# Up projections that sum both activation halves into the same 256 PSUM columns

## What is computed

```
# block 1: gated, with a 3-tap convolution along the sequence, D_FF = 5632
h2 = rmsnorm(x, norm_ffn[l])
u = h2 @ w_up[l]                      # 256 x 2048 @ 2048 x 11264
up = jnp.pad(u, ((0, 0), (1, 1), (0, 0)))
u = up[:, :-2] * cw[0] + up[:, 1:-1] * cw[1] + up[:, 2:] * cw[2] + conv_b[l]
gate, val = jnp.split(u, 2, axis=-1)
x = x + (jax.nn.silu(gate) * val) @ w_down[l]
...
# block 2: square of a relu, D_FF_2 = 8192
# u = rms_norm(x) @ w_up_2 ; act = relu(u) ** 2 ; y = act @ w_down_2
```

## Time and profile before

| | |
|---|---|
| timed runs | 2583.70, 2588.72, 2589.14 us; median 2588.72 us |
| profiled execution, first to last instruction (span) | 2586.3 us |
| PE busy | 2532.6 us (98%) |
| DVE, ACT busy | 1524.2 us (59%), 1224.6 us (47%) |

### The profile page before, as it was taken

One profiled execution on the slowest core, in us unless ns is written; L12 is line 12 of the kernel. 1 busy time (PEld: TensorE's weight loads), 2 busy tenths in 40 slices (PEclk: granted clock), 3 DMA queues, 4 the chain that ended last, 5 costly groups with the idle time before them and its releaser, 6 DMA issues.

```text
span 2586.3 us, 32846 instructions
## 1 busy us (share of the span) xinstructions
PE 2532.6 (98%) x12492; PEld 2125.8 (82%) x12492; DVE 1524.2 (59%) x1719; ACT 1224.6 (47%) x1540; POOL 49.7 (2%) x71
## 2 busy tenths in 40 slices
PE   7999999999999999999999999999899999999997
PEld 6888888878888888888877887788788888888886
DVE  4665656655776467756765346655565565565555
ACT  5444456544655355534544344444544343443443
POOL 0100100000000000000000000000000000000000
PEclk9999999999999999999999999999999999999999
DMA  7665455655555555555546455445465555555553
GB/s 257 192 194 178 150 168 167 224 176 180 181 182 191 189 185 190 184 195 181 192 163 235 144 168 159 155 151 175 146 196 194 181 192 190 186 185 192 182 205 114
DMA packets 249926, 469.96 MB, mean 182 GB/s; under 512 B 22320, under 2 KB 25648, under 8 KB 249184
## 3 DMA queue, kind: packets, MB, share of 16 engines
q1 hardware_dynamic: 249824, 468.58, 55.2%
HBM read 466.42 MB, written 2.13 MB: 181 GB/s over the span
## 4 chain that ended last, share of the span: by engine, by line
PE 96%; DVE 2%; ACT 1%; issue 0%; DMA 0%; POOL 0%; SPq 0%; POOLq 0%; DVEq 0%; ACTq 0%
PE psum L1580 21%; PE psum L1542 19%; PE psum L1544 19%; PE psum L1543 19%; PE psum L1581 10%; PE psum L1584 1%; PE psum L1657 1%; PE psum L1670 1%; PE psum L1593 1%; PE psum L1583 1%; PE psum L1642 1%; PE psum L1819 1%; DVE wl L1012 0%; DMA raw<-in_w_in 0%; ACT wh L613 0%
## 5 line engine op out<-in xcount | busy, mean ns | idle before, releaser
L1012 DVE TENSOR_TENSOR wl<-raw,wh 128x1024 fp32r<-128x1024 f32 x856 | 1048.9, 1226 | 966.4 <-ACT wh L613 961.3
L613 ACT ACTIVATE wh<-raw 128x1024 fp32r<-128x1024 f32 x856 | 904.1, 1058 | 1046.0 <-PE psum L1544 621.6
L1542 PE MATMUL psum<-wh,ha 128*128 128x512 f32 x1728 | 697.1, 403 | 8.9 <-DVE wl L1012 8.5
L1544 PE MATMUL psum<-wh,ha 128*128 128x512 f32 x1728 | 676.4, 391 | 0.0
L1543 PE MATMUL psum<-wl,ha 128*128 128x512 f32 x1728 | 674.8, 391 | 0.0
L1580 PE MATMUL psum<-ha,wh 128*128 128x512 f32 x1320 | 465.9, 398 | 5.0 <-DVE x_rows L1221 4.5
L1542 PEld LDWEIGHTS psum<-wh,ha 128*128 128x128 f32 x1728 | 325.9, 189 | 76.0 <-issue 10.7
L1544 PEld LDWEIGHTS psum<-wh,ha 128*128 128x128 f32 x1728 | 325.4, 188 | 70.8
L1543 PEld LDWEIGHTS psum<-wl,ha 128*128 128x128 f32 x1728 | 326.1, 189 | 66.2
L1581 PE MATMUL psum<-ha,wl 128*128 128x256 f32 x1320 | 370.1, 280 | 0.0
L1580 PE MATMUL psum<-hb,wh 128*128 128x512 f32 x960 | 339.4, 398 | 5.2 <-DVE rows L1520 3.2
(11 more groups left out here) (211 smaller groups left out, 1416.2 us busy)
## 6 DMA issues: line engine op xcount, KB each, us to landing
raw<-in_w_up SPq DMA_DIRECT2D x152, 1024.0 KB, 5.0
raw<-in_w_in SPq DMA_DIRECT2D x120, 1024.0 KB, 5.1
raw<-in_w_down SPq DMA_DIRECT2D x108, 1024.0 KB, 4.9
raw<-in_w_out SPq DMA_DIRECT2D x32, 1024.0 KB, 5.0
raw<-in_w_branch_a SPq DMA_DIRECT2D x8, 1024.0 KB, 5.0
raw<-in_w_branch_b SPq DMA_DIRECT2D x8, 1024.0 KB, 4.9
x_rows<-in_x SPq DMA_DIRECT2D x4, 512.0 KB, 9.4
bias<-in_b_rpb SPq DMA_DIRECT2D x32, 64.0 KB, 6.8
```

What stands on the lines that cost most here:

```text
L613: act.activation(wh[q % SPLIT_SLOTS][:], raw[q // 2 % RAW_SLOTS][:, 2 * (q % 2):2 * (q % 2) + 2, :], ACT.Copy).then_inc(hi_done, 1)
L1012: dve.tensor_tensor(wl[q % SPLIT_SLOTS][:], raw[q // 2 % RAW_SLOTS][:, 2 * (q % 2):2 * (q % 2) + 2, :], wh[q % SPLIT_SLOTS][:].bitcast(F32 ...
L1542: pe.matmul(acc, hi, wh[s][:, c, :], start=first and c == 0, stop=False)
L1544: ins = pe.matmul(acc, lo, wh[s][:, c, :], start=False, stop=last and c == 1)
```

## The change

Each couple becomes three matmuls of 256 columns into the same 256 sums: hi weights x high activations, hi weights x low activations, lo weights x high activations. Two groups of channels share a bank, so a channel block needs 2 banks and a pair needs 4 (banks 0 to 3 for all channel blocks). Down passes use banks 4 to 7, but for the third one of block 1, which stays in banks 0 to 3. The copy of the left halves on ACT is gone; DVE takes the sums out and scales them in one instruction (in block 2 with the relu in it), and the square is an instruction of its own. PE no longer waits for `row_free` before later up passes, nor for the copy of the 1/rms row before the second channel block, nor for `chan_free` before the down passes other than that third one.

```diff
+    def half_bank(ffn, v):
+        return 2 * (1 - v) if ffn == 1 else 2 * v
+
+    def half(ffn, v):
+        b = half_bank(ffn, v)
+        return psum[:, b:b + 2, :].rearrange("p b (d s) -> p (b d) s", s=SEQ)
+
+    def row_bank(g):
+        high = R_DOWN1[0] <= g < R_DOWN1[2] or g >= R_DOWN2[0]
+        return (4 if high else 0) + 2 * (g % 2)
...
# ACT, up1_stage (the later stages move up by one)
-            if j == 0:
-                act.wait_ge(sem["cmask_in"], 4)
-                act.wait_ge(mm_done, S_UP1[p] + 8 * v + 8 + 16 * i)
-
-                act.activation(u_pad[v][:, :, 1:SEQ + 1], psum[:, 4 * v:4 * v + 4, 0:SEQ], ACT.Copy
-                               ).then_inc(sem["half_ok"], 1)
-            if j == 2:
-                act.wait_ge(sem["u_scaled"], v + 1 + 2 * pair)
+            if j == 1:
+                act.wait_ge(chan_free, FREE + 2 * pair + v + 1)
...
# DVE, up1_stage
             if j == 0:
-                dve.wait_ge(sem["half_ok"], count)
-                u = u_pad[v][:, :, 1:SEQ + 1]
-                dve.tensor_tensor(u, psum[:, 4 * v:4 * v + 4, SEQ:2 * SEQ], u, ALU.add).then_inc(chan_free, 1)
-            if j == 1:
-                dve.wait_ge(chan_free, FREE + count)
+                dve.wait_ge(mm_done, S_UP1[p] + 8 * v + 8 + 16 * i)
                 dve.wait_ge(sem["rstd_row_ok"], 1)
-                u = u_pad[v][:, :, 1:SEQ + 1]
-                dve.tensor_tensor(u, u, rstd_row[:].unsqueeze(1).to_broadcast([P, 4, SEQ]), ALU.mult
-                                  ).then_inc(sem["u_scaled"], 1)
+                dve.tensor_tensor(u_pad[v][:, :, 1:SEQ + 1], half(1, v),
+                                  rstd_row[:].unsqueeze(1).to_broadcast([P, 4, SEQ]), ALU.mult
+                                  ).then_inc(chan_free, 1)
...
# PE, channel_step
                 for d in range(4):
-                    acc = psum[:, 4 * v + d, :]
                     hi, lo = (w[s][:, c, P * d:P * d + P] for w in (wh, wl))
-                    if k < KC - 1:
-                        pe.matmul(acc, hi, both, start=k == 0, stop=False)
-                        ins = pe.matmul(acc[:, 0:SEQ], lo, src[:, k, 0, :], start=False, stop=False)
-                    else:
-                        pe.matmul(acc[:, 0:SEQ], lo, src[:, k, 0, :], start=False, stop=False)
-                        ins = pe.matmul(acc, hi, both, start=False, stop=True)
+                    pe.matmul(acc[:, d, :], hi, src[:, k, 0, :], start=k == 0 and d % 2 == 0, stop=False,
+                              skip_group_check=True)
+                    pe.matmul(acc[:, d, :], hi, src[:, k, 1, :], start=False, stop=False, skip_group_check=True)
+                    ins = pe.matmul(acc[:, d, :], lo, src[:, k, 0, :], start=False, stop=k == KC - 1,
+                                    skip_group_check=True)
...
# PE, channel_blocks and first_pair
-            pe.wait_ge(row_free, FREE + rows_before)
             with pe.Fori(0, n) as i:
...
-            pe.wait_ge(row_free, FREE + rows_before)
+            pe.wait_ge(row_free, FREE + rows_before - 1)
...
-            row_of_roots(count)
-            pe.wait_ge(sem["rstd_row_ok"], count)
+            row_of_roots(ffn)
+            pe.wait_ge(row_free, FREE + rows_before)
```

More of the change, by code:

```diff
@@ L800, in up1_stage @@
                 ins.then_inc(sem["conv_mid"], 1)
-            if j == 5 and v == 0:
+            if j == 4 and v == 0:
                 act.wait_ge(sem["conv_done"], 1 + 2 * pair)
                 act.activation(conv[0][:], conv[0][:], ACT.Silu).then_inc(sem["silu_done"], 1)
-            if j == 6 and v == 1:
+            if j == 5 and v == 1:
                 act.wait_ge(sem["act_ready"], pair + 1)
@@ L831, in tail @@
                 if b == 0 and j < 4:
-                    for stage in ((0, 1), (2, 3), (4, 5), (6,))[j]:
+                    for stage in ((0, 1), (2, 3), (4,), (5,))[j]:
                         up1_stage(p, stage, 1, j0 + n - 1, n - 1)
@@ L965, in up2_stage @@
         def up2_stage(j, c, i):
[L967 to L971, removed]
+            if j == 2:
                 act.wait_ge(sem["act_ready"], 11 + c + 1 + 4 * i)
@@ L1219, in evac @@
                 d = dst[:, :, bass.ds((b + m * i) * COLS, COLS)]
+                acc = psum[:, row_bank(g):row_bank(g) + 2, :]
                 if add:
-                    dve.tensor_tensor(d, psum[:, 2 * (g % 2):2 * (g % 2) + 2, :], d, ALU.add).then_inc(row_free, 1)
+                    dve.tensor_tensor(d, acc, d, ALU.add).then_inc(row_free, 1)
                 else:
-                    dve.tensor_copy(d, psum[:, 2 * (g % 2):2 * (g % 2) + 2, :]).then_inc(row_free, 1)
+                    dve.tensor_copy(d, acc).then_inc(row_free, 1)
             return evac
@@ L1259, in up1_stage @@
                     dve.wait_ge(sem["tap_done"], count)
-                tap = 0 if j == 3 else 2
+                tap = 0 if j == 2 else 2
                 for s in range(4):
@@ L1264, in up1_stage @@
                                                    par[:, bass.ds(w, 1)], conv[v][:, s, :], ALU.mult, ALU.add)
-                ins.then_inc(sem["tap_done" if j == 3 else "conv_done"], 1)
-            if j == 5 and v == 1:
+                ins.then_inc(sem["tap_done" if j == 2 else "conv_done"], 1)
+            if j == 4 and v == 1:
                 dve.wait_ge(sem["conv_done"], count)
@@ L1477, in up2_stage @@
             if j == 0:
-                dve.wait_ge(sem["usum_done"], c + 1 + 4 * i)
-                dve.tensor_tensor(u_sum[:], psum[:, 4 * (c % 2):4 * (c % 2) + 4, SEQ:2 * SEQ], u_sum[:], ALU.add
-                                  ).then_inc(chan_free, 1)
+                dve.wait_ge(mm_done, S_UP2[0] + 8 * (c % 4 + 1) + 64 * (c // 4) + 64 * i)
+                dve.wait_ge(sem["rstd_row_ok"], 2)
+                dve.scalar_tensor_tensor(u_sum[:], half(2, c % 2), 0.0,
+                                         rstd_row[:].unsqueeze(1).to_broadcast([P, 4, SEQ]), ALU.max, ALU.mult
+                                         ).then_inc(chan_free, 1)
             if j == 1:
                 dve.wait_ge(chan_free, FREE + C_UP2[0] + c + 1 + 4 * i)
[L1483 to L1490, removed]
+                dve.tensor_tensor(u_act[:], u_sum[:], u_sum[:], ALU.mult).then_inc(sem["act_ready"], 1)
+            if j == 3:
                 dve.wait_ge(sem["hb_hi"], 11 + c + 1 + 4 * i)
@@ L1751, in _ @@
             if p == 0:
-                first_pair(S_UP1[0], C_UP1[0], ha, T_FFN1, 1, rows_before, last_group)
-            channel_blocks(S_UP1[p] + 16 * peeled, C_UP1[p] + 2 * peeled, n - peeled, ha, rows_before)
-            pe.wait_ge(chan_free, FREE + C_UP1[p] + 2 * n - 1)
+                first_pair(1, S_UP1[0], C_UP1[0], ha, T_FFN1, R_DOWN1[0], last_group)
+            channel_blocks(1, S_UP1[p] + 16 * peeled, C_UP1[p] + 2 * peeled, n - peeled, ha)
+            if p == 0:
+                pe.wait_ge(sem["rstd_row_ok"], 1)
+            if p == 2:
+                pe.wait_ge(chan_free, FREE + C_UP1[p] + 2 * n - 1)
             enter = next_input(T_MIX2, R_DOWN1[p])
             def down_hook(b, j):
-                if p == 2 and b:
-                    if b == 1 and j == 1:
-                        pe.wait_ge(chan_free, FREE + 22)
+                if b == 0 and j == 2 * n - 1:
+                    pe.wait_ge(chan_free, FREE + 22)
+                if b:
                     enter(b, j)
             row_blocks(S_DOWN1[p], R_DOWN1[p], 4, 2 * n, hb, hb_by(j0, 4), extra=down_hook if p == 2 else None)
-            rows_before = R_DOWN1[p] + 4
         def four_transposes(bank, src, rows=P):
```

35 lines of the change are left out of this document (17 added, 18 removed).

## The result

The changed kernel takes 2596.72 us (median of nine runs, 2593.68 to 2598.61), the kernel before 2587.92 us (nine runs beside it, 2582.98 to 2589.14). The ratio is 1.0038, with a 95% interval of 1.0029 to 1.0047: slower by 0.4%. The prediction was 2596, slower.

A forecast was written before the change was run, and what follows sets the result against it. PE was taken to bound the kernel, busy 2532.6 of 2586.3 us. Terms +19.5 - 10.9 - 1.3 = +7.3 us give a span of 2593.6; with the median 2.4 us above the span, 2596 us, range 2576 to 2622.

The forecast's parts named there:

- Three matmuls for two: In the up passes, three matmuls of 256 take 360 ns against 352 for a couple, over 2432 couples: +19.5 us.
- The seam: Where chunk 14 meets chunk 15, two matmuls of 256 follow each other, starting 120 ns apart; the forecast took this price.
- The waits: PE's removed stops: -10.9 us ahead of up passes and -1.3 us for the 1/rms row.
- rival D: At heads of up passes a late split or evacuation catches PE and the 12.2 us stay: 2608 us; chance 0.1.
- The down passes: PE has no wait for the activation chain in a down pass; its shortening means nothing gained, nothing lost.
- B: In the up passes each matmul pays the slower beat's 16.6 ns: stream +43.8 us, kernel 2620 us; chance 0.2.
- C: In channel_step splitting a 512 costs nothing: the stream stays at 856 us, the waits are gained, 2576 us; chance 0.2.

The follow-up runs named there:

- the split alone: The kernel before with only its couples made three matmuls of 256 columns; banks, waits and evacuations as before: 2606.37 us, ratio 1.0079.

## Why the prediction was right

**The path.** PE bound the kernel and still does, and the work that DVE and ACT lost does not shorten it.

**Three matmuls for two, +19.5 us forecast.** 360.0 ns a place as forecast. Without the slow starts the second stretch before had 351.5 ns and all couples about 351.8, so the term is 8.2 x 2432 = +19.9 us. Alone on the chip it is 2606.37 - 2586.91 = +19.5 by the medians, and 17 to 24 by the interval of the ratio. The step that carried it was to take the price of a matmul from distances over many of them (226.7 for a 512, 346.9 for a couple at the faster beat) and not from the rows of the 256s inside couples. The seam at the earlier trace rows gave the same 120 and was the only direct sight of it.

**The waits, -12.2 us forecast.** By the profile: five heads at 1.98 - 0.22 = 1.76 us, the first at 1.71 - 0.23 = 1.48, two roots at 1.08 - 0.36 = 0.72, and the slow starts behind the six heads, 0.1 each. Behind the row of roots a slow start is left: the first 256 takes 0.20 us instead of 0.12. That makes 8.8 + 1.5 + 1.4 + 0.6 = 12.3 us less. Put back on the chip the waits cost 11.9. PE is not caught late in an up pass, so rival D was wrong.

**The down passes: a step that was wrong by 0.8 us.** The prediction says that PE has no wait for the activation chain in a down pass and that nothing is lost there. The kernel before has one, the 4.1 us for `hb` shown above. The third down pass of block 1 follows three pairs and not four and has six steps in a block, so PE comes to the last activations after 11.06 us, while they are ready 15.18 us after the up pass has ended. In the changed kernel the chain is a stage shorter, and they are ready after 16.00 us. DVE's rows in the two kernels show where it waits:

```profile
1302.14 1.22 DVE L1012 TENSOR_TENSOR wl<-raw,wh 128x1024 fp32r<-128x1024 f32 x1
1304.37 1.68 DVE L1263 SCALAR_TENSOR_TENSOR conv<-u_pad,par,conv 128x256 f32<-128x256 f32 x4 [1.01 <-ACT conv L798]
```

```profile
1310.30 1.23 DVE L1016 TENSOR_TENSOR wl<-raw,wh 128x1024 fp32r<-128x1024 f32 x1 [3.10 <-ACT wh L627]
1311.44 3.37 DVE L1265 SCALAR_TENSOR_TENSOR conv<-u_pad,par,conv 128x256 f32<-128x256 f32 x8
```

The up pass ended at 1297.25 and at 1303.49, so the taps of the convolution begin 7.12 us behind it before and 7.95 us now. In the changed kernel they stand behind a split in DVE's program, and that split waits 3.10 us for ACT, which works on `conv` first. All ten profiles with the old evacuation have 15.2 us here, all four with the new one 16.0. The wait costs more than its length, in either kernel: in the 4.1 us behind it the granted clock was 0.59 of full speed before and 0.50 now, and the row matmuls that run at the lower of the clock's two levels start 0.43 us apart instead of 0.23. Up to the next up pass the two profiles differ by only 0.07 us (557.73 and 557.80), a stretch that varies between 554.1 and 557.8 in the profiles of these kernels, so the 0.8 us do not stand out in it.

**The sum.** The first two terms give +7.6; the medians differ by 8.8 and the spans by 9.5. Of the last 2 us, 0.6 were there before the first up pass began (622.09 - 1.48 = 620.61 before, 621.20 after), and 0.9 in the first up pass of block 2 (93.4 us became 95.6, where 256 places and the removed waits account for 1.3). No run takes these apart, and the runs of one kernel differ by 5 us. That the time itself was met within 0.7 us is in part luck: the forecast started from a median of 2588.7 us, and nine runs have 2587.92.

**The rivals.** B's slower beat did not appear: all streams of 256s ran at 120.0 ns, and only streams that change width showed it. C's point, that a 512 splits for nothing, is refuted by the split alone. The 109 ns that it cited are those of plain f32 rows, their columns plus 2 ns; the fp32r rows do not share that. The rule that the prediction cited from the Trainium skill ("TensorE: Matmul & The Clock Gate", section "Back-to-back issue gap", columns / 2.4 + 2.5 ns) would have made the three matmuls an estimated 327.5 ns; the trace has 360.0. The page gives that rule for isolated matmuls, not for a stream of weight loads and matmuls.

What the profile of before held and the prediction passed over: it did not ask where the faster beat comes from. It was found nearly always behind the long stop at a head, so the waits had a value as well as a price. For the changed kernel that makes no difference; for one that keeps the 512s it was 2.7 us.

## What to carry to other kernels

Where PE is the bound, count matmuls as well as columns: here each fp32r matmul of 256 or 512 columns costs its columns at 2.4 GHz plus 13.3 ns, so a split of wide matmuls that frees PSUM must save that for each one added (8 ns here, where the couples had a surplus of their own). Ask first whether the banks can be handed over in another way: swapping the roles of the halves from pass to pass removed five of the six waits at the heads and kept the wide matmuls, and with the order of widths it gave 0.73% where the change lost 0.38%. Look too for the one pass that is shorter than the others: a chain that is hidden in most passes can be in the open there, and a shorter chain can still end later. Read the price of a thing from totals of long uniform stretches, and look for one place in the trace where two of the new kind already stand side by side.

## What the runs showed of the hardware that was not expected

Streams of fp32r matmuls of one width are steady: 226.7 ns for 512 columns, 120.0 for 256, about 112 for 128, all with weights of 128 columns. Streams that change between 512 and 256 have a surplus over 226.7 + 120.0 = 346.7 ns that depends on the order: 0 or 6.3 to 6.6 ns with alternation (two beats, the faster one nearly always only behind a stop of about 2 us; with the 256 first it lasts the whole stretch, with the 512 first one or two channel blocks), 4.1 in runs of four (3.3 in one stretch), 2.4 in runs of eight, 1.6 in runs of two as 256, 512, 512, 256. What sets this surplus stays open, as does the cause of the 13.3 ns. Whether one matmul can add both halves of a 512 into the same 256 sums, which would keep the couples and halve the banks, was not tried.
